# Long-convolution mixer: z weights' low halves to GpSimd, a z unit split around the last sum, a table write on another queue

## The chip, the cores and the metric

The kernel runs on one core of one Trainium2 chip. The metric is the device time of one execution in microseconds. Engines are named as in the profile: PE (TensorE), PEld (its weight loads), DVE (VectorE), ACT (ScalarE), POOL (GpSimd) and SP (SyncE, which here only issues DMAs).

## The reference

The whole reference is a stack of four mixers (long convolution, forgetting attention, short convolution, long convolution) and one block of three attentions and a feed-forward layer, all on 256 positions of 1024 channels in float32. The change touches the long-convolution mixer, which runs first and fourth:

```
def conformer_conv_mixer(h, w_in, conv_w, conv_b, ln_g, ln_b, w_out):
    proj = h @ w_in
    val, glu_gate, z = jnp.split(proj, 3, axis=-1)
    u = val * jax.nn.sigmoid(glu_gate)
    u = causal_depthwise_conv(u, conv_w) + conv_b
    u = jax.nn.silu(layer_norm(u, ln_g, ln_b))
    return (u * jax.nn.silu(z)) @ w_out
```

Here h is 256 x 1024, val, glu_gate and z are 256 x 2048 each, and the convolution has 31 taps on each of 2048 channels. It touches one thing more: a table of relative-position biases that an attention of the last block reads. The kernel builds it at its start and writes it, shifted 16 times, to a DRAM tensor `skew` (28 rows of 16 copies of 384 floats, 0.69 MB), from which it is read at about 1182 us.

## The kernel before

**Units, halves and the ring.** Weights stream from DRAM in units of 256 columns (two halves of 128 columns, 1 MB a unit) through a ring of three buffers. SP issues the loads in order; before it loads unit u it waits until unit u-3 has been used up: by PE for a plain unit, or by the engines that split it for a split unit. A plain unit goes to PE as float32 (L596, in `proj_T`). A split unit is cut into a high part (`whi`, an ACT cast, L362) and a low part (`wlo`, the unit minus its high part, L371 in `lo_to`), and PE forms three products for each tile (L598 to L600). `whi` and `wlo` hold four halves. With the flag `dve` of `unit_in` true, the half with an even number in the whole program has its low part made by DVE and the other by POOL; with the flag false both are POOL's. In the first call of the mixer the even half of a unit is its first, in the second call its second.

**The loop of the mixer.** There are 16 chunks c of 128 channels. `vg` unit c (plain) holds val and gate of chunk c; a `z` unit (split) comes after every fourth of them (z units 0 to 3), and z units 4 to 7 come after the loop. For each chunk ACT applies the sigmoid (L743), DVE multiplies (`gated`, L846) and then does 20 of the 31 taps (L873, L871, L876). ACT multiplies the other 11 taps into four buffers `tmp` (L764) and POOL adds them up (L819, nine adds, and a last one L822 that increments `pool_sum`). ACT may be at most four taps ahead of POOL. DVE joins both parts (`join`, L853 and L854): chunk c-1 is joined after DVE's taps of chunk c, so that POOL has a chunk's time to spare, except for chunk 15, which is joined as soon as DVE's own taps of it and the join of chunk 14 are done. The order on each engine is fixed by the program text. `sigmoid(c+1)`, with the casts that it runs ahead of need (`act_ahead`), stands in chunk c of ACT behind three taps. `conf_z(i)` is SiLU of z unit i with a table load (L728); for i = 0, 1, 2 it stands at the head of `sigmoid` of chunk 4, 8, 12, for i = 3 behind the loop. DVE's low parts stand behind `gated(c+1)` in chunk c, POOL's between its third and fourth add of chunk c. For z unit 3 that is chunk 13, for z unit 4 chunk 14. PE may be at most two units ahead of the engine that empties its bank.

**The statistics.** The layer norm needs the sum (L925, `sum_of`) and the sum of squares (L931, `squares_of`, of squares made by ACT, L749) over all 16 chunks, by PE with a matrix of ones. DVE's first operation on the finished sums is L894. Then come the centring (L900, L915), SiLU (L789), the product with z on POOL (L831) and the output product (L634 to L636), in a fixed interleaving with z units 5 to 7.

**The start.** In the first call POOL also issues the four DMAs of `write_skew` (L797) at the head of its chunk 2. For chunks 0 to 2 a shift is computed and DVE waits for it (L768 on ACT, L886 on DVE) behind ACT's taps of chunk 2.

Of the kernel before, what the change touches and what calls it, by code (L numbers as in the profile page):

```python
# [24 lines left out]
P = 128  # L25
# [4 lines left out]
E = 2048  # L30
# [73 lines left out]
def program(nc, t, out):  # L104
    ctx = ExitStack()
    with ctx:
# [276 lines left out]
        def group(free):  # L383
            groups.append(free)
            return len(groups) - 1
# [34 lines left out]
        def plan_conf(ph, j):  # L420
            w = t["a_w_in"][j]
            n = {"ph": ph, "j": j}
            n["vg"], n["z"] = [], []

            def z_group(i):
                n["z"].append((group((sz_done, j * 8 + i + 1)), unit_in(w, [(2 * E + i * 2 * P, 2 * P)], True)))

            for c in range(KE):

                n["vg"].append((group((u_done, j * KE + c + 1)), unit_in(w, [(c * P, P), (E + c * P, P)], plain=True)))  # L430
                if c % 4 == 3:
                    z_group(c // 4)
            for i in range(4, 8):
                z_group(i)
            n["out"] = plan_out(t["a_w_out"][j], KE)
            return n
# [142 lines left out]
                mm = nc.tensor.matmul(out, ll, rh, start=False, stop=(i == n - 1))  # L579
            return mm  # L580

        def proj_T(pe, g, u, first=False, ph=0):

            b = take_bank(pe, g)
            for a, h in enumerate(hs(u)):
                o = b[:, a * S:(a + 1) * S]
                if is_split(h):
                    split_ready(pe, h)
                    wh, wl = piece(whi, h), piece(wlo, h)
                else:  # L590
                    landed(pe, u)
                for k in range(KD):
                    if first and a == 0:
                        pe.wait_ge(xn_done, 4 * ph + k // 2 + 1)
                    if not is_split(h):
                        mm = nc.tensor.matmul(o, halves[h][1][:, k, :], sqb[:, k, :], start=(k == 0), stop=(k == KD - 1))  # L596
                        continue
                    nc.tensor.matmul(o, wh[:, k, :], xh[:, k, :], start=(k == 0), stop=False)  # L598
                    nc.tensor.matmul(o, wh[:, k, :], xl[:, k, :], start=False, stop=False)  # L599
                    mm = nc.tensor.matmul(o, wl[:, k, :], xh[:, k, :], start=False, stop=(k == KD - 1))  # L600
                mm.then_inc(half_done, 1)
# [129 lines left out]
        def conf_act(act, n):  # L731
# [20 lines left out]
            for c in range(KE):  # L752
                act.wait_ge(u_done, j * KE + c + 1)
                for i in range(TAPS_POOL):
                    if i == TAPS_POOL // 3 and c + 1 < KE:
                        sigmoid(c + 1)
                    if i == 2 * TAPS_POOL // 3 and c >= 3:
                        square(c - 3)
                    k = TAPS_DVE + i
                    m = (j * KE + c) * TAPS_POOL + i  # L760
                    wait(act, tap_done, m - 3)
                    src = up[:, c % 3, k:k + S]
                    bias = cols[:, ROWB + j * KE + c:ROWB + j * KE + c + 1] if i == 0 else 0.0
                    nc.scalar.activation(tmp[:, m % 4, :], src, ACT.Identity, scale=taps[:, j, k, c:c + 1],  # L764
                                         bias=bias).then_inc(tmp_done, 1)
                if c == 2:
                    act.wait_ge(m0_done, j + 1)
                    nc.scalar.activation(shift, bank[2][:, 0:S], ACT.Copy, scale=-1.0 / P).then_inc(shift_done, 1)  # L768
            conf_z(act, n, 3)
            square(KE - 3)  # L770
            act_ahead(act, n["z"][4][1])
            square(KE - 2)
# [16 lines left out]
                nc.scalar.activation(yb[:, c, :], yb[:, c, :], ACT.Silu, scale=lg, bias=lb).then_inc(act_done, 1)  # L789
            out_act(act, n)  # L790

        def write_skew(pool):

            pool.wait_ge(tab_copied, 4)
            for v, (h0, nh) in enumerate(((0, 16), (16, 4), (20, 4), (24, 4))):
                src = tabs[0:nh, v, :].unsqueeze(1).to_broadcast((nh, COPIES, TABLE))
                pool.dma_start(skew[h0:h0 + nh, :, :], src).then_inc(skew_written, 16)  # L797

        def conf_pool(pool, n):
            j = n["j"]  # L800
            for c in range(KE):
                if j == 0 and c == 2:
                    write_skew(pool)
                first = (j * KE + c) * TAPS_POOL
                for i in range(2, TAPS_POOL):
                    if i == TAPS_POOL // 2 and c + 1 < KE:
                        lo_pool_to(pool, ahead(n["vg"][c + 1][1]))
                    to = accp[:, c % 2, i % 2, :]
                    pool.wait_ge(tmp_done, first + i + 1)
                    if i == 2 and c >= 2:  # L810
                        if c < 5:
                            pool.wait_ge(raw_done, 3 * j + c - 1)
                        else:
                            pool.wait_ge(conv_done, j * KE + c - 1)
                    if i >= 4:
                        pool.wait_ge(tap_done, first + (1 if i == 4 else 4 if i == 5 else i - 1))
                    a = tmp[:, (first + i - 2) % 4, :] if i < 4 else to

                    nc.gpsimd.tensor_tensor(to, a, tmp[:, (first + i) % 4, :], ALU.add)\  # L819
                        .then_inc(tap_done, 3 if i == 3 else 1)  # L820
                pool.wait_ge(tap_done, first + TAPS_POOL)
                nc.gpsimd.tensor_tensor(accp[:, c % 2, 0, :], accp[:, c % 2, 0, :], accp[:, c % 2, 1, :], ALU.add).then_inc(pool_sum, 1)  # L822
            lo_pool_to(pool, ahead(n["z"][4][1]))
            for c in range(KE):
                if c in Z_BESIDE:
                    lo_pool_to(pool, ahead(n["z"][Z_BESIDE[c]][1]))
                if c in OUT_BESIDE:
                    lo_pool_to(pool, ahead(n["out"][OUT_BESIDE[c]][2]))
                pool.wait_ge(act_done, j * KE + c + 1)
                wait(pool, sz_done, j * 8 + c // 2 + 1)  # L830
                nc.gpsimd.tensor_tensor(y_slot(pool, n["y0"] + c), yb[:, c, :], zb[:, c, :], ALU.mult).then_inc(y_raw, 1)  # L831
            lo_pool_to(pool, last(n["out"][-1][2]))
# [87 lines left out]
        def conf_pe(pe, n):  # L920
# [24 lines left out]
            for c in range(KE - 4, KE - 2):  # L945
                sum_of(c)
                squares_of(c - 2)
            for c in range(KE - 2, KE):
                sum_of(c)
                squares_of(c - 2)  # L950
            for c in range(KE - 2, KE):
                squares_of(c)
            for i in range(5, 8):
                proj_T(pe, *n["z"][i])
            out_pe(pe, n, y_hi, y_lo, KE, y_split, n["y0"])

# [981 lines left out]
        def _(sp):  # L1938
# [25 lines left out]
            for u, (_, parts) in enumerate(units):  # L1964
                if u >= RING:
# [4 lines left out]
                        wait(sp, lo_pool, n_hi[h] - n_dve(h))  # L1970
                    else:
                        sp.wait_ge(half_done, h + 1)
                for nk, at, width, src in parts:
                    sp.dma_start(raw(u, nk)[:, :, at:at + width], src).then_inc(unit_loaded[u % RING], 16)

# [128 lines left out]
```

## Time and profile before

| | |
|---|---|
| median of 3 runs | 1704.94 us (1703.66 to 1708.4) |
| profiled execution, its own time | 1704.73 us |
| its span in the trace | 1702.9 us |
| first call of the mixer | about 37 to 292 us of the span |
| second call | about 852 to 1098 us |
| PE, DVE, ACT, POOL busy | 94%, 55%, 50%, 44% of the span |
| mean granted TensorE clock | 0.975 |

Times of instructions below are microseconds from the start of the span. In a row of the timeline the bracket is the idle time of that engine just before it, with what ended it. PE's busy share counts overlapping entries, so that its idle time is read from those brackets. Both calls run the same program; from chunk 3 on their rows stand 811.8 us apart, within a microsecond.

### The profile page before, as it was taken

How to read it: one execution, taken by the hardware profiler on the slowest of the kernel's cores; microseconds unless marked ns; L12 is line 12 of the kernel's file. 1: busy time of each engine (PE TensorE's matmuls, PEld its weight loads, DVE VectorE, ACT ScalarE, POOL GpSimd, SP SyncE). 2: the span in 40 equal slices, each digit the busy share in tenths (PEclk: the TensorE clock that was granted, in tenths of full speed). 3: DMA queues.
4: the chain of work that ended last, by engine and by line, in shares of the span. 5: the costliest groups of instructions: out<-in, count | busy, mean ns of one | idle time of the engine just before them, and what ended most of it. 6: DMA issues, size and time to landing. Idle time of an engine off the chain costs nothing.

```text
span 1702.9 us, 28287 instructions
## 1 busy us (share of the span) xinstructions
PE 1593.6 (94%) x10947; PEld 1454.9 (85%) x10947; DVE 934.9 (55%) x2023; ACT 855.7 (50%) x1526; POOL 741.6 (44%) x572
## 2 busy tenths in 40 slices
PE   4999878999999989999899988899999999889998
PEld 3888778998788989999888878898887778889998
DVE  3799965444565554444379998423035545633332
ACT  2577764553455444444357776443325646444442
POOL 0688853332222424444258895365411112334432
PEclk8999989999999999999999999999999999999999
DMA  4654435446553546766444434675752112646654
GB/s 127 143 146 135 130 108 175 133 165 127 122 123 124 163 135 177 195 175 197 124 124 137 136 128 138 152 186 140 182 153 71 51 56 86 194 136 177 187 156 125
DMA packets 341453, 240.11 MB, mean 141 GB/s; under 512 B 36925, under 2 KB 328475, under 8 KB 341320
## 3 DMA queue, kind: packets, MB, share of 16 engines
q1 hardware_dynamic: 329880, 231.33, 47.7%
q10 hardware_dynamic: 10992, 6.29, 1.7%
q0 software_dynamic: 448, 0.69, 0.5%
q8 instruction: 87, 1.43, 0.4%
q14 instruction: 46, 0.38, 0.1%
HBM read 236.55 MB, written 1.74 MB: 140 GB/s over the span
## 4 chain that ended last, share of the span: by engine, by line
PE 70%; DVE 17%; ACT 5%; issue 4%; POOL 2%; DMA 1%; SPq 1%; DVEq 0%; POOLq 0%; ACTq 0%
PE bank L598 8%; DVE bank L876 8%; PE bank L599 8%; PE bank L600 8%; PE bank L634 4%; PE bank L636 4%; PE bank L635 4%; PE bank L990 4%; PE bank L1288 3%; PE bank L596 3%; PE bank L1289 3%; PE bank L1290 3%; PE bank L610 2%; DVE wlo L371 2%; PE bank L1083 1%
## 5 line engine op out<-in xcount | busy, mean ns | idle before, releaser
L371 POOL TENSOR_TENSOR wlo<-ring,whi 128x1024 fp32r<-128x1024 f32 (+3 forms) x210 | 481.7, 2295 | 786.0 <-ACT whi L362 785.9
L362 ACT CAST whi<-ring 128x1024 fp32r<-128x1024 f32 (+4 forms) x389 | 379.2, 990 | 274.8 <-PE bank L600 106.2
L598 PE MATMUL bank<-xh,whi 128*128 128x256 f32 x1384 | 402.4, 291 | 32.4 <-DVE xl L562 19.4
L371 DVE TENSOR_TENSOR wlo<-ring,whi 128x1024 fp32r<-128x1024 f32 (+3 forms) x179 | 254.6, 1423 | 267.0 <-ACT whi L362 266.1
L599 PE MATMUL bank<-xl,whi 128*128 128x256 f32 x1384 | 397.0, 287 | 0.0
L600 PE MATMUL bank<-xh,wlo 128*128 128x256 f32 x1384 | 396.7, 287 | 0.0
L598 PEld LDWEIGHTS bank<-xh,whi 128*128 128x128 f32 x1384 | 271.2, 196 | 42.3 <-issue 39.8
L599 PEld LDWEIGHTS bank<-xl,whi 128*128 128x128 f32 x1384 | 271.6, 196 | 0.2
L600 PEld LDWEIGHTS bank<-xh,wlo 128*128 128x128 f32 x1384 | 271.2, 196 | 0.0
L819 POOL TENSOR_TENSOR scratch<-scratch 128x256 f32<-128x256 f32 x288 | 211.3, 766 | 127.0 <-ACT scratch L764 123.1
L596 PE MATMUL bank<-sqb,ring 128*128 128x256 f32 x1024 | 230.1, 385 | 17.3 <-DVE xl L562 9.7
L596 PEld LDWEIGHTS bank<-sqb,ring 128*128 128x128 f32 x1024 | 196.9, 193 | 47.2 <-issue 10.5
L876 DVE SCALAR_TENSOR_TENSOR bank<-scratch,convw,bank 128x256 f32<-128x256 f32 x576 | 231.1, 482 | 0.0
L764 ACT ACTIVATE scratch<-scratch,convw 128x256 f32<-128x256 f32 x320 | 147.2, 500 | 61.3 <-POOL scratch L819 60.4
L634 PE MATMUL bank<-y_hi,whi 128*128 128x256 f32 x512 | 150.0, 293 | 9.3 <-POOL wlo L371 4.3
L636 PE MATMUL bank<-y_hi,wlo 128*128 128x256 f32 x512 | 147.0, 287 | 0.0
L635 PE MATMUL bank<-y_lo,whi 128*128 128x256 f32 x512 | 146.9, 287 | 0.0
L1288 PE MATMUL bank<-xh,whi 128*128 128x256 f32 x384 | 110.6, 288 | 1.4 <-DVE qk L1251 0.8
L634 PEld LDWEIGHTS bank<-y_hi,whi 128*128 128x128 f32 x512 | 100.5, 196 | 11.7 <-DVE y_lo L714 4.2
L1289 PE MATMUL bank<-xl,whi 128*128 128x256 f32 x384 | 108.6, 283 | 0.0
L1290 PE MATMUL bank<-xh,wlo 128*128 128x256 f32 x384 | 108.5, 283 | 0.0
L635 PEld LDWEIGHTS bank<-y_lo,whi 128*128 128x128 f32 x512 | 100.4, 196 | 0.2
(254 smaller groups left out, 2640.5 us busy)
## 6 DMA issues: line engine op xcount, KB each, us to landing
ring<-in_a_w_in_dram SPq DMA_DIRECT2D x64, 512.0 KB, 5.2
ring<-in_b_w_in_dram SPq DMA_DIRECT2D x32, 1024.0 KB, 5.8
ring<-in_c_w_in_dram SPq DMA_DIRECT2D x64, 512.0 KB, 5.4
ring<-in_w_in_dram SPq DMA_DIRECT2D x26, 1024.0 KB, 5.4
ring<-in_w_ffn_in_dram SPq DMA_DIRECT2D x44, 512.0 KB, 5.1
ring<-in_a_w_in_dram SPq DMA_DIRECT2D x16, 1024.0 KB, 5.3
ring<-in_a_w_out_dram SPq DMA_DIRECT2D x16, 1024.0 KB, 5.0
ring<-in_w_ffn_out_dram SPq DMA_DIRECT2D x16, 704.0 KB, 4.5
```

What stands on the lines that cost most here:

```text
L362: nc.scalar.copy(piece(whi, h)[:, :, 0:n], src).then_inc(hi_done, 1)
L371: engine.tensor_tensor(piece(wlo, h)[:, :, 0:n], src, piece(whi, h)[:, :, 0:n].bitcast(F32), ALU.subtract).then_inc(done, 1)
L596: mm = nc.tensor.matmul(o, halves[h][1][:, k, :], sqb[:, k, :], start=(k == 0), stop=(k == KD - 1))
L598: nc.tensor.matmul(o, wh[:, k, :], xh[:, k, :], start=(k == 0), stop=False)
L599: nc.tensor.matmul(o, wh[:, k, :], xl[:, k, :], start=False, stop=False)
L600: mm = nc.tensor.matmul(o, wl[:, k, :], xh[:, k, :], start=False, stop=(k == KD - 1))
L634: nc.tensor.matmul(o, wh[:, k, :], hi[:, kk, :], start=first, stop=False, skip_group_check=True)
L635: nc.tensor.matmul(o, wh[:, k, :], lo[:, kk, :], start=False, stop=False, skip_group_check=True)
L636: mm = nc.tensor.matmul(o, wl[:, k, :], hi[:, kk, :], start=False, stop=end, skip_group_check=True)
L819: nc.gpsimd.tensor_tensor(to, a, tmp[:, (first + i) % 4, :], ALU.add)\
L876: ins = nc.vector.scalar_tensor_tensor(to[:, a, :], src, w, to[:, a, :], ALU.mult, ALU.add)
L1288: nc.tensor.matmul(o, wh, xh[:, k, :], start=first, stop=False, skip_group_check=True)
```

## The change

Five edits:

1. z units 0, 1, 2, 3 and 5: the flag is false, so POOL makes both low parts. z units 4, 6 and 7 keep one half on DVE.
2. `conf_z(3)` moves from behind ACT's loop into chunk 15, behind three of its 11 taps. It brings the cast of the first half of z unit 5 with it. The `hi_to` that is added behind the taps finds that half cast already.
3. POOL makes the low part of z unit 5's first half directly behind its last chunk; as before, the next halves follow.
4. On PE the first half of z unit 5 comes between the sum of chunk 14 with the squares up to chunk 13 and the sum of chunk 15; the second half comes behind the last squares. The order was: all sums and squares, then the whole unit.
5. `write_skew` is issued by SP, just ahead of the load of `vg` unit 4, instead of by POOL.

```
-                n["z"].append((group((sz_done, j * 8 + i + 1)), unit_in(w, [(2 * E + i * 2 * P, 2 * P)], True)))
+                n["z"].append((group((sz_done, j * 8 + i + 1)), unit_in(w, [(2 * E + i * 2 * P, 2 * P)], i == 4 or i > 5)))
...
-        def proj_T(pe, g, u, first=False, ph=0):
+        def proj_T(pe, g, u, first=False, ph=0, only=(0, 1)):
-            b = take_bank(pe, g)
+            b = take_bank(pe, g) if 0 in only else bank[g % 2]
             for a, h in enumerate(hs(u)):
+                if a not in only:
+                    continue
...
-                    if i == TAPS_POOL // 3 and c + 1 < KE:
-                        sigmoid(c + 1)
+                    if i == TAPS_POOL // 3:
+                        if c + 1 < KE:
+                            sigmoid(c + 1)
+                        else:
+                            conf_z(act, n, 3)
...
+                if c == KE - 1:
+                    hi_to(act, hs(n["z"][5][1])[0])
...
-            conf_z(act, n, 3)
             square(KE - 3)
...
-        def write_skew(pool):
-            pool.wait_ge(tab_copied, 4)
+        def write_skew(sp):
+            sp.wait_ge(tab_copied, 4)
...
-                pool.dma_start(skew[h0:h0 + nh, :, :], src).then_inc(skew_written, 16)
+                sp.dma_start(skew[h0:h0 + nh, :, :], src).then_inc(skew_written, 16)
...
-                if j == 0 and c == 2:
-                    write_skew(pool)
...
+            lo_pool_to(pool, hs(n["z"][5][1])[0])
             lo_pool_to(pool, ahead(n["z"][4][1]))
...
-            for c in range(KE - 2, KE):
-                sum_of(c)
-                squares_of(c - 2)
+            sum_of(KE - 2)
+            squares_of(KE - 4)
+            squares_of(KE - 3)
+            proj_T(pe, *n["z"][5], only=(0,))
+            sum_of(KE - 1)
             for c in range(KE - 2, KE):
                 squares_of(c)
-            for i in range(5, 8):
+            proj_T(pe, *n["z"][5], only=(1,))
+            for i in range(6, 8):
...
+                if u == conf0["vg"][4][1]:
+                    write_skew(sp)
```

## Rows read from the trace of the kernel before

**Rows 1.** The page: busy time, share of the span and instructions of each engine.
```profile
PE 1593.6 (94%) x10947; PEld 1454.9 (85%) x10947; DVE 934.9 (55%) x2023; ACT 855.7 (50%) x1526; POOL 741.6 (44%) x572
```

**Rows 2.** The chain that ended last, first call: start, length, what.
```profile
80.54 3.59 DVE bank L876 x10
...
152.53 7.17 PE bank L596 x32
```

**Rows 3.** Timeline of DVE, first call, chunk 13 and behind the loop.
```profile
179.63 1.72 DVE L371 TENSOR_TENSOR wlo<-ring,whi 128x1024 fp32r<-128x1024 f32 x1
...
206.07 4.52 DVE L371 TENSOR_TENSOR wlo<-ring,whi 128x1024 fp32r<-128x1024 f32 x2
210.51 0.41 DVE L894 TENSOR_SCALAR rr<-bank 128x256 f32<-128x256 f32 x1
```

**Rows 4.** Timeline of PE, first call; the bracket is idle time before.
```profile
73.41 7.07 PE L596 MATMUL bank<-sqb,ring 128*128 128x256 f32 x32
...
82.67 7.17 PE L596 MATMUL bank<-sqb,ring 128*128 128x256 f32 x32 [1.75 <-ACT wide L728]
...
189.03 0.59 PE L931 MATMUL bank<-scratch,cst 128*128 128x256 f32 x2
...
205.12 1.22 PE L925 MATMUL bank<-wide,cst 128*128 128x256 f32 x2 [4.47 <-DVE wide L854]
```

**Rows 5.** Waits of PE, first call, 90 to 160: total us, times, longest.
```profile
PE bank L596 <- DVE scratch L846: 3.0, 2, 2.1
PE bank L598 <- DVE wlo L371: 0.6, 1, 0.6
```

**Rows 6.** Timeline of POOL, first call, chunks 13 and 15.
```profile
177.90 2.37 POOL L371 TENSOR_TENSOR wlo<-ring,whi 128x1024 fp32r<-128x1024 f32 x1
...
197.65 6.24 POOL L819 TENSOR_TENSOR scratch<-scratch 128x256 f32<-128x256 f32 x9
203.96 0.73 POOL L822 TENSOR_TENSOR scratch<-scratch 128x256 f32<-128x256 f32 x1
```

**Rows 7.** POOL's adds by tile, 174 to 206: duration ns min/median/max.
```profile
L819 POOL TENSOR_TENSOR scratch<-scratch x27: 721/733/1724, 174.7 to 203.2; 128x256 f32<-128x256 f32 x27
```

**Rows 8.** Timeline of ACT, first call: sigmoid of chunk 4, and chunk 15.
```profile
83.93 0.39 ACT L743 ACTIVATE scratch<-bank 128x256 f32<-128x256 f32 x1
...
196.20 0.51 ACT L764 ACTIVATE scratch<-scratch,convw 128x256 f32<-128x256 f32 x1 [0.19 <-POOL scratch L819]
...
201.84 1.03 ACT L362 CAST whi<-ring 128x1024 fp32r<-128x1024 f32 x1
202.89 1.28 ACT L728 ACT_TABLE_LOAD   x1
204.18 0.60 ACT L728 ACTIVATE wide<-bank 128x512 f32<-128x512 f32 x1
```

**Rows 9.** Timeline of POOL, first call: issue of the table write.
```profile
72.06 2.56 POOL L797 DMA_DIRECT2D skew<-qk  x4
```

**Rows 10.** Timeline of SP's queue, first call: issue of `vg` unit 4's load.
```profile
60.31 0.99 SPq L1974 DMA_DIRECT2D ring<-in_a_w_in_dram  x2
```

**Rows 11.** DMA issues, 70 to 76: what, count, KB each, median us to landing.
```profile
skew<-qk POOLq DMA_DIRECT2D x1, 384.0 KB, 5.8
skew<-qk POOLq DMA_DIRECT2D x3, 96.0 KB, 15.0
```

**Rows 12.** The chain, second call: matmuls at the two clock levels.
```profile
1049.35 0.21 PE bank L635
...
1055.01 0.12 PE bank L635
```

**Rows 13.** Timelines of DVE and POOL, second call.
```profile
891.34 0.75 DVE L886 TENSOR_TENSOR wide<-wide,bank 128x256 f32<-128x256 f32 x2 [0.35 <-ACT bank L768]
...
1015.73 0.73 POOL L822 TENSOR_TENSOR scratch<-scratch 128x256 f32<-128x256 f32 x1
...
1021.55 0.42 DVE L894 TENSOR_SCALAR rr<-bank 128x256 f32<-128x256 f32 x1 [1.69 <-PE bank L931]
```

## The prediction

> **What bounds the kernel now.** The page first: PE is busy 94% of the span and DVE 55% [rows 1], so an engine at half load can matter only in a stage where the others wait for it. The chain of waits shows where: in the first call it runs on DVE's taps from 80.54 us to near 150, touches PE at 152.53 [rows 2], and then changes between PE, ACT and POOL until 205. The second call reads alike. So the loop looks bound by DVE; the question is how far behind it the others are.
>
> PE: from 152.53 (four `vg` units and z unit 3, with their sums) it works without a wait until 189.5 [rows 2, 4], 36.9 us for four chunks. In the first call it waited only 2.1 us before `vg` unit 8, 0.9 before `vg` unit 12 (3.0 in two waits, the longest 2.1) and 0.6 for a DVE low part in between [rows 5]. So four chunks of DVE with one low part take 36.9 + 0.9 = 37.8 us, and PE is 0.9 behind.
>
> POOL: the sum of chunk 15 ends at 203.96 + 0.73 = 204.69 [rows 6], which I call T. PE sums chunk 14 at 205.12, after a wait for the join of chunk 14, which ended at about 205.0 [rows 4]; the join of chunk 15 follows directly. So at the end of the loop POOL is within half a microsecond of DVE. In chunk 15 it has no chunk to spare. This small distance decides more than DVE's load.
>
> After T: DVE's first operation on the statistics, which I call S, is at 210.51 in the first call, T + 5.8 [rows 3, 6], and at 1021.55 in the second, T + 5.1 with T = 1015.73 + 0.73 [rows 13]. Everything that follows is ordered behind S: normalising, SiLU, the products, and in between the casts and low parts of z units 6 and 7 that PE waits for. So a shift of S is taken as a shift of the end of the call, and a shift of T is one of S.
>
> **The change, step by step** (plus is later).
>
> *Low parts of z units 1 to 3.* DVE loses about 1.7 us for each [rows 3], 5.1 per call. But PE permits only part: over a cycle of four chunks 0.9 instead of 1.7. POOL gains a low part of 2.37 [rows 6] and loses something: one of its adds takes 1.72 instead of 0.73 [rows 7], just where DVE's low part runs beside it, at 179.63 to 181.35 [rows 3, 7]. So POOL pays 2.37 - 0.99 = +1.4 for each. Away from the end POOL has a chunk to spare. In chunk 13 it hasn't: with chunks 13, 14 and 15 it runs straight to T. There: +1.4.
>
> The Trainium skill (SBUF - State Buffer, section "Who interferes with whom") says that a DVE instruction with two SBUF inputs and a GpSimd instruction that reads SBUF block each other for a whole instruction. The 1.72 of the trace agrees with it. By it POOL's price would be 2.37 less up to 1.7, so +0.7 instead of +1.4.
>
> *`conf_z(3)` in chunk 15.* Behind ACT's third tap (ends 196.7) come a cast of 1.03, a table load of 1.28 and SiLU of 0.60 [rows 8], 2.9 in all; the fourth tap ends at about 200.0, where POOL's second add used to start at 197.65 + 0.7 = 198.35 [rows 6]. So +1.65 on T. That SiLU's set also serves the taps is taken from the loop, where no load stands between them; else 1.3 more. Behind the loop ACT has 2.9 less to do, which hid beside PE: worth nothing.
>
> *The start.* POOL's chunk 1 gets +1.4 for z unit 0. In the first call its chunk 2 loses the 2.56 of the DMA issues [rows 9]: together -1.2, and DVE waits for ACT and POOL there. In the second call nothing is removed: DVE's wait was 0.35 [rows 13] and it would itself be earlier, so +1.4 less a little, +1.3.
>
> *The table write on SP's queue.* The load of `vg` unit 4 was issued at 60.31 [rows 10] and PE used it from 73.41 [rows 4]. Now four writes stand ahead of it. Before, they were issued from 72.06, and three of them took 15.0 us to land [rows 11]: 16 from first issue to last landing. The load now lands between 60.3 + 13.7 = 74 (the write's last bytes overlap with the load) and 60.3 + 16 + 3.7 = 80 (nothing overlaps, a load's bytes behind it). I take the middle, 77. Then PE is idle 3.6 us, and begins `vg` unit 4 at the low clock, as after the 4.47 idle before 205.12, when a sum took twice its time [rows 4]: +1.6. PE ends it at about 86.0 instead of 80.9, and `vg` unit 5 starts at 86.0 instead of 82.67, +3.3. ACT's sigmoid of chunk 4 was at 83.93 [rows 8], now 86.0: +2.1 there and about +1.7 for DVE.
>
> *Sum up to T.* First call: before `vg` unit 8 PE is at 3.3 - 2.1 - 0.6 = +0.6, DVE at 1.7 - 1.7 = 0: PE decides. Before unit 12 PE is at 0.6 - 0.9 = -0.3, DVE at -1.7. Chunk 13 of POOL hangs on PE's unit 13, so -0.3, and T is at -0.3 + 1.4 + 1.65 = +2.7. With the table write hidden the same walk from -1.2 gives -2.9 at unit 8 and -3.8 at unit 12, so T = -0.8; with a landing at 80, +5.7. Second call: from +1.3, -0.4 at unit 8, -1.3 at unit 12, so T = +1.7, with bounds of 0 and +3.
>
> *From T to S.* PE now does z unit 5's first half before the last sum. Its low part begins at T on POOL: 2.37, and up to 1.0 more if DVE's low part of z unit 6 blocks it. Then 24 matmuls, at 0.12 or 0.21 each [rows 12]: 2.9 or 5.1. Then a sum and two squares, 0.43 each at the high clock (0.59 less what overlaps [rows 4]) or 0.85: 1.3 or 2.6. With 0.1 for the hand-over, S is at T + 6.7 to T + 11.2. PE is idle ahead of T as before (4.47), so I take the low clock for the half and the high one behind it: 2.37 + 0.1 + 5.1 + 1.3 = T + 8.9. First call 8.9 - 5.8 = +3.1 (from +0.9 to +5.4), second 8.9 - 5.1 = +3.8 (from +1.6 to +5.1). What DVE saves (the 4.52 of two low parts becomes one [rows 3]) is hidden by this. That PE has half a unit less to do behind S is worth nothing: it waits there for ACT's and POOL's casts and low parts of z units 6 and 7.
>
> Sum: 2.7 + 3.1 + 1.7 + 3.8 = +11.3. The profiled execution took 1704.73, the median is 1704.94; both give 1716.
>
> **Rivals.**
>
> *The write is hidden and the half runs at the high clock:* -0.8 + 0.9 + 1.7 + 1.6 = +3.4, 1708. For it: the load had 7 us of slack. Against it: the 15.0 us.
>
> *Faster:* DVE stays the bound because POOL catches up. It decides if POOL ends its sum of chunk 15 at least 2.4 us before DVE's joins, so that the low part of the half is ready at the join. Then T would be -1.2 - 5.1 in the first call, +1.3 - 5.1 in the second, S stays where it is behind T: -10, 1695. Against it: POOL is within 0.5 us of DVE now and its chunks 13 and 15 get longer.
>
> *The three small writes one after another,* not side by side: each of the second and third adds most of 10 us more, PE starts `vg` unit 4 near 95, and the first call is some 15 us later still: about 1732. Each of the three reads only four partitions; in the trace they ran together, so this isn't seen. The Trainium skill (DMA: Bandwidth & Descriptors, section "Why a DMA increments its semaphore by 16 and not by 1") has a rule that would bring it about: writes of four rows issued by SP all go to the same lowest-numbered four DMA engines, those issued by GpSimd to the next ones in turn; no run here shows it.
>
> **How the numbers follow.** Forecast (POOL's end and the half before the last sum make it slower, the write partly exposed): 0.62, its own range 1710 to 1723. Hidden write and high clock, 1708: 0.18. Faster, 1695: 0.12. Writes in series: 0.08. Leaving out the faster case and most of the series case, the range is 1702 to 1724. About 0.3% (5.1 us) is what a measurement tells from no change. Slower by more: 0.62 + 0.08, 0.70; the 1708 case lies within, 0.18; faster 0.12.
>
> **What would show it.** In the profile after: POOL's L822 of chunk 15 no earlier than 204 in the first call and 1017 in the second, relative to their starts; DVE idle before the join of chunk 15, waiting for L822; PE waiting for POOL's `wlo` before the first half of z unit 5; S at T + 7 to 11; PE idle before `vg` unit 4 with `ring` late. The prediction is wrong if DVE still has no idle time before the last join, if PE has z unit 5's low part at hand when chunk 14 is joined, or if L596 at about 73.4 starts on time: then the first rival's terms apply.

## The result, and the profile after

After the change the kernel takes 1720.78 us (median of 4 runs, 1718.25 to 1721.86), beside 1706.67 us for the kernel before in all of its 4 runs so far (1703.66 to 1708.59). The ratio is 1.0082, with an interval of 1.006 to 1.0104: slower, by 14 us. The profiled execution took 1721.85 us, its span is 1720.0, 17.1 more than before.

The page, busy time of each engine, and the chain of work that ended last by engine:

```profile
PE 1601.1 (93%) x10947; PEld 1461.6 (85%) x10947; DVE 916.6 (53%) x2013; ACT 855.1 (50%) x1526; POOL 754.1 (44%) x578
...
PE 76%; DVE 8%; ACT 6%; issue 4%; POOL 3%; SPq 1%; DMA 1%; ACTq 0%; DVEq 0%; POOLq 0%
```

Beside [rows 1] DVE has 18.3 us less to do and POOL 12.5 more. That is what the change does, and it says nothing of the end. Two marks of each call do: T, the end of POOL's sum of chunk 15, and S, the start of DVE's first operation on the statistics. Here both are counted from the reciprocal of the normalisation ahead of the call (L558 on DVE, at 33.46 and 847.39 us in the trace of before, 33.53 and 858.06 after), so that what happened earlier in the kernel drops out.

| us | before | after | more |
|---|---|---|---|
| first call: T | 171.2 | 178.0 | +6.8 |
| first call: T to S | 5.8 | 9.2 | +3.4 |
| first call: to the next stage's L558 | 259.7 | 269.8 | +10.1 |
| second call: T | 169.1 | 171.2 | +2.1 |
| second call: T to S | 5.1 | 8.4 | +3.3 |
| second call: to the next stage's L558 | 252.4 | 257.0 | +4.6 |
| the attention stages, from there to the last L558 | 398.8 | 401.4 | +2.6 |

**Where the first call's 6.8 us come from.** SP's queue and PE, around the load of `vg` unit 4 (before: [rows 10, 4]):

```profile
60.45 8.35 SPq L803 DMA_DIRECT2D skew<-qk  x4
68.84 7.70 SPq L1984 DMA_DIRECT2D ring<-in_a_w_in_dram  x2
```

```profile
81.25 9.49 PE L598 MATMUL bank<-sqb,ring 128*128 128x256 f32 x32 [7.75 <-DMA ring<-in_a_w_in_dram]
```

The chain of work in that stretch (start, length, what) names each step:

```profile
60.45 0.69 SPq L803
...
61.18 0.70 SPq L803
...
61.92 3.08 SPq L803
...
65.04 3.76 SPq L803
...
68.84 3.69 SPq L1984
...
72.58 8.53 DMA ring<-in_a_w_in_dram
```

POOL issued the same four DMAs in 2.56 us [rows 9]. On SP the first two are short, and then each issue takes 3 to 4 us, the load's own two included (3.69 and 3.96). The view by windows says why. Its columns are the window, its length, busy time (and instructions) of PE, PEld, DVE, ACT and POOL, the granted clock, the share of the 16 DMA engines that was busy, and GB/s:

```profile
62.00:65.00 3.00, 3.00 (x15) 2.65 (x14) 3.00 (x9) 2.50 (x7) 2.43 (x3) 1.00 0.90 102
66.00:69.00 3.00, 3.00 (x21) 2.79 (x20) 2.96 (x9) 0.00 (x0) 3.00 (x3) 1.00 0.22 26
```

```profile
65.00:69.00 4.00, 4.00 (x25) 3.68 (x24) 3.93 (x11) 0.03 (x1) 4.00 (x3) 1.00 0.31 36
69.00:73.00 4.00, 4.00 (x36) 4.00 (x35) 2.34 (x7) 3.00 (x7) 3.92 (x7) 1.00 0.24 30
73.00:77.00 4.00, 0.50 (x5) 0.29 (x3) 3.87 (x10) 2.84 (x7) 4.00 (x7) 0.85 0.58 123
77.00:81.00 4.00, 0.00 (x0) 0.00 (x0) 3.06 (x9) 3.77 (x8) 3.92 (x7) 0.50 0.82 239
```

From 62 to 65 us the large write (384 KB, from 16 partitions) moves 102 GB/s. From 66 to 69 the share is 0.22, which is 3.6 of 16 DMA engines, and 26 GB/s move (from 69 to 73 an instruction fetch on another queue raises the figures to 0.24 and 30). The three small writes are 96 KB each, [rows 11], which at 26 GB/s is 3.8 us each. That is about the length of one held issue, and three of them, 11.4 us, reach from the large write's end near 65.6 to about 77. So the reading is that they run one behind the other on about four DMA engines, and that SP is held in its issues meanwhile. PE ran out of work at 73.5, and at 77 it is at 0.50 of its clock, the 1.2 GHz level; its `vg` unit 4 then takes 9.49 us instead of 7.07.

**Where the 3.3 us from T to S come from.** PE, POOL and DVE in the first call (before: [rows 4, 6, 3]):

```profile
206.52 1.22 PE L930 MATMUL bank<-wide,cst 128*128 128x256 f32 x2 [3.71 <-DVE wide L859]
...
213.98 0.55 PE L600 MATMUL bank<-xh,whi 128*128 128x256 f32 x1 [3.61 <-POOL wlo L371]
...
219.19 0.59 PE L930 MATMUL bank<-wide,cst 128*128 128x256 f32 x2
```

```profile
205.22 5.51 POOL L823 TENSOR_TENSOR scratch<-scratch 128x256 f32<-128x256 f32 x8 [1.76 <-ACT scratch L769]
210.81 0.73 POOL L826 TENSOR_TENSOR scratch<-scratch 128x256 f32<-128x256 f32 x1
211.49 5.66 POOL L371 TENSOR_TENSOR wlo<-ring,whi 128x1024 fp32r<-128x1024 f32 x2
```

```profile
205.59 0.42 DVE L858 TENSOR_TENSOR wide<-bank,scratch 128x256 f32<-128x256 f32 x1
...
211.63 0.42 DVE L858 TENSOR_TENSOR wide<-bank,scratch 128x256 f32<-128x256 f32 x1 [5.17 <-POOL scratch L826]
...
212.61 2.30 DVE L371 TENSOR_TENSOR wlo<-ring,whi 128x1024 fp32r<-128x1024 f32 x1
220.76 0.42 DVE L899 TENSOR_SCALAR rr<-bank 128x256 f32<-128x256 f32 x1 [5.84 <-PE bank L936]
```

DVE joins chunk 14 at 205.59 and then stands idle for 5.17 us until POOL's last sum (T = 211.54). PE stands idle for 3.61 until POOL has the low part of z unit 5's first half, at 213.98 it begins that half, and only at 219.19 does it sum chunk 15, whose join was ready at 212.5. So the last sum starts 6.7 us after its join is ready, behind 24 matmuls that nobody needs yet. The second call shows the same:

```profile
1029.36 0.42 DVE L858 TENSOR_TENSOR wide<-bank,scratch 128x256 f32<-128x256 f32 x1 [5.13 <-POOL scratch L826]
...
1037.65 0.42 DVE L899 TENSOR_SCALAR rr<-bank 128x256 f32<-128x256 f32 x1 [7.41 <-PE bank L936]
```

### The profile page after: what moved, and what is told of

Same layout as the page of the kernel before. It is cut to its first block, busy times and chain, and to the rows that moved or that the text cites. A ratio compares the mean times of both kernels' runs of the same rounds, so it can differ in the third digit from the quotient of the medians.

```text
span 1720.0 us, 28288 instructions
## 1 busy us (share of the span) xinstructions
PE 1601.1 (93%) x10947; PEld 1461.6 (85%) x10947; DVE 916.6 (53%) x2013; ACT 855.1 (50%) x1526; POOL 754.1 (44%) x578
## 4 chain that ended last, share of the span: by engine, by line
PE 76%; DVE 8%; ACT 6%; issue 4%; POOL 3%; SPq 1%; DMA 1%; ACTq 0%; DVEq 0%; POOLq 0%
PE bank L598 9%; PE bank L600 9%; PE bank L601 8%; PE bank L602 8%; PE bank L636 4%; PE bank L638 4%; PE bank L637 4%; PE bank L998 4%; PE bank L1296 3%; PE bank L1297 3%; PE bank L1298 3%; PE bank L612 2%; ACT whi L362 2%; POOL scratch L823 1%; PE bank L1091 1%
## 5 line engine op out<-in xcount | busy, mean ns | idle before, releaser
L371 POOL TENSOR_TENSOR wlo<-ring,whi 128x1024 fp32r<-128x1024 f32 (+3 forms) x220 | 505.5, 2302 | 785.2 <-ACT whi L362 784.9
L602 PE MATMUL bank<-xh,wlo 128*128 128x256 f32 x1384 | 399.1, 288 | 0.0
L371 DVE TENSOR_TENSOR wlo<-ring,whi 128x1024 fp32r<-128x1024 f32 (+3 forms) x169 | 236.4, 1399 | 269.4 <-ACT whi L362 268.6
L823 POOL TENSOR_TENSOR scratch<-scratch 128x256 f32<-128x256 f32 x288 | 202.9, 738 | 128.6 <-ACT scratch L769 128.4
```

The source lines that it names most:

```text
L371: engine.tensor_tensor(piece(wlo, h)[:, :, 0:n], src, piece(whi, h)[:, :, 0:n].bitcast(F32), ALU.subtract).then_inc(done, 1)
```

## The experiments

Each was run beside the kernel before on the same chip. T and S are as above, first call / second call, from one profile of each kernel.

| run | median us | ratio to before | T | T to S |
|---|---|---|---|---|
| after | 1720.78 | 1.0082 [1.006, 1.0104] | 178.0 / 171.2 | 9.2 / 8.4 |
| e1: after, write on POOL | 1714.8 | 1.005 [1.0036, 1.0064] | 173.4 / 171.0 | 8.6 / 8.3 |
| e2: after, z unit 5 whole | 1710.08 | 1.0032 [1.002, 1.0045] | 178.0 / 170.5 | 4.1 / 3.6 |
| e3: after, SiLU behind the loop | 1716.07 | 1.006 [1.0047, 1.0073] | 175.9 / 168.9 | 8.5 / 8.5 |
| e4: after, z unit 3 shared | 1716.16 | 1.0063 [1.005, 1.0076] | 176.2 / 169.9 | 7.3 / 8.9 |
| e5: before, write on SP | 1712.16 | 1.0037 [1.0025, 1.0049] | 177.8 / 169.2 | 5.9 / 5.1 |
| e6: before, split alone | 1709.81 | 1.0026 [1.0018, 1.0035] | 171.2 / 169.3 | 7.8 / 7.9 |
| e7: before, other placement | 1698.49 | 0.9956 [0.9944, 0.9968] | 165.9 / 167.1 | 5.7 / 4.4 |
| e8: before, loop part alone | 1699.08 | 0.9966 [0.9953, 0.9978] | 165.8 / 167.0 | 5.8 / 4.9 |
| e9: after, write behind the load | 1714.18 | 1.005 [1.0034, 1.0066] | 170.6 / 171.2 | 9.2 / 8.4 |
| e10: e7, z unit 6's low part later | 1695.93 | 0.9948 [0.9934, 0.9961] | 165.9 / 166.9 | 4.2 / 5.2 |
| e11: e1 and e2 together | 1705.48 | 0.9999 [0.9991, 1.0008] | 173.3 / 171.2 | 4.1 / 3.0 |

### One part of the change undone (e1 to e4)

**e1**, the write issued by POOL again:

```
-                if u == conf0["vg"][4][1]:
-                    write_skew(sp)
...
+                if j == 0 and c == 2:
+                    write_skew(pool)
```

> The changed kernel with one part undone: the table is again written from GpSimd's queue at the head of its chunk 2. T is the end of POOL's last sum in a call, S DVE's first operation on the finished sums, both counted from DVE's first reciprocal of the call. Main theory (the write stands ahead of the load of vg unit 4, PE idles 7.8 us and runs that unit at the low clock): PE does not wait for the ring before vg unit 4, T of the first call falls from 178.0 to about that of a call without the write, 173.5, S from 187.2 to 182.5; the whole is 4 to 5 us less than the changed kernel, about 1716. The second call does not move. Rival (the write is hidden behind the slower chain of POOL, and the wait before unit 4 costs nothing by chunk 15): T of the first call stays near 178, the time near 1720.

T came back by 4.6 us in the first call and by next to nothing (0.2) in the second; by the ratios the kernel is 0.0032 shorter, 5.5 us (the two intervals touch, 1.0064 and 1.006). `vg` unit 4 was on time in PE:

```profile
74.49 7.17 PE L598 MATMUL bank<-sqb,ring 128*128 128x256 f32 x32
```

So the write on SP's queue is the first call's largest term, and the mechanism is the late load. T is still 2.2 us later than before, as in the second call (1.9 here).

**e2**, z unit 5 whole, behind all sums:

```
-            proj_T(pe, *n["z"][5], only=(0,))
             sum_of(KE - 1)
...
-            proj_T(pe, *n["z"][5], only=(1,))
-            for i in range(6, 8):
+            for i in range(5, 8):
```

> The changed kernel with PE's order of before: all sums and squares first, then z unit 5 whole. Main theory (the last sum and squares wait behind the half of z unit 5, which waits for POOL's low part): T stays in both calls (178.0 and 171.2 from the call's start), S comes at T + 3 to 4 instead of T + 9.2 and T + 8.4, since the join of chunk 14 is long done and only one sum and two squares are left behind T; 5 to 6 us less in each call, 10 to 11 in all, about 1710. Rival (the half only fills time in which the squares wait for ACT, and S is set by DVE's low part and ACT's squares): S moves by 1 to 2, the time stays within 3 us of 1720.

T stayed (178.0, and 170.5 for 171.2), and S came to T + 4.1 and T + 3.6, 5.1 and 4.8 us less. DVE, first call:

```profile
211.85 0.42 DVE L858 TENSOR_TENSOR wide<-bank,scratch 128x256 f32<-128x256 f32 x1 [5.17 <-POOL scratch L826]
...
212.83 2.31 DVE L371 TENSOR_TENSOR wlo<-ring,whi 128x1024 fp32r<-128x1024 f32 x1
215.83 0.42 DVE L899 TENSOR_SCALAR rr<-bank 128x256 f32<-128x256 f32 x1 [0.70 <-PE bank L936]
```

DVE now makes its one low part and finds the statistics 0.70 us behind it. The half ahead of the last sum costs 9.9 us by the marks and 8.5 by the ratios (1.0082 less 1.0032), the largest part of the whole. That is more than the 3.4 and 3.3 of the table above, because without the split S would have come 1.7 and 1.5 us nearer to T than before. In the first call it was DVE's two low parts that set T + 5.8, [rows 3], and one of them is gone. In the second call of before DVE had one low part there and then waited 1.69 us for PE, [rows 13], which had the sums of chunk 14 and of chunk 15 behind T; now chunk 14's are done by T, because T comes 5 us after DVE is ready.

**e3**, the cast and SiLU of z unit 3 behind ACT's loop, and **e4**, a half of z unit 3 on DVE:

```
# e3
-                    if i == TAPS_POOL // 3:
-                        if c + 1 < KE:
-                            sigmoid(c + 1)
-                        else:
-                            conf_z(act, n, 3)
+                    if i == TAPS_POOL // 3 and c + 1 < KE:
+                        sigmoid(c + 1)
...
-                if c == KE - 1:
-                    hi_to(act, hs(n["z"][5][1])[0])
...
+            conf_z(act, n, 3)
# e4
-  ... unit_in(w, [(2 * E + i * 2 * P, 2 * P)], i == 4 or i > 5)))
+  ... unit_in(w, [(2 * E + i * 2 * P, 2 * P)], i in (3, 4) or i > 5)))
```

> The changed kernel with SiLU of z unit 3 (conf_z(3)) behind ACT's loop again. Main theory (the cast, the table load and the SiLU inside chunk 15 hold up ACT's fourth tap and with it POOL by 1.65 us): T is 1.6 to 1.8 earlier in both calls, S follows, since PE waits for POOL's low part after T: 3.3 less in all, about 1717.5. Rival (DVE or PE, not POOL, sets T): T does not move. Rival (ACT is too busy behind the loop with it, so that the squares become late): T moves but S does not.

> The changed kernel with z unit 3 shared between DVE and POOL again (flag true), z units 0, 1, 2, 5 as changed. Main theory (from chunk 13 on POOL runs straight to T, and a second low part there costs it 2.37 less the 1.0 that it loses beside DVE's low part): T is 1.4 earlier in both calls, S follows, 2.8 less in all, about 1718; DVE's idle time before the last join falls by about 3. Rival by the lock rule taken fully (0.7 per low part): 1.4 less in all. Rival (POOL has time to spare): T stays.

T came back by 2.1 and 2.3 us with e3, by 1.8 and 1.3 with e4; the ratios by 0.0022 and 0.0019, 3.8 and 3.2 us. The intervals of these ratios overlap with that of after, so the reading rests on T, which moved in both calls. Both say the same of chunks 13 to 15: POOL runs straight to T there, and what ACT or POOL gets more to do arrives at T. With e3, ACT's work between its third and fourth tap is gone. In the trace of after it reads as ACT and the gap on POOL:

```profile
201.74 1.03 ACT L362 CAST whi<-ring 128x1024 fp32r<-128x1024 f32 x1
202.79 1.28 ACT L730 ACT_TABLE_LOAD   x1
204.09 0.60 ACT L730 ACTIVATE wide<-bank 128x512 f32<-128x512 f32 x1
204.58 0.90 ACT L769 ACTIVATE scratch<-scratch,convw 128x256 f32<-128x256 f32 x2
```

No table load stands ahead of the taps at 204.58, as the prediction had taken from the loop. In e4 DVE's idle time before the last join fell from 5.17 to 1.45 us, and the first call's T to S from 9.2 to 7.3, which was not expected. There PE had been idle for only 0.81 us ahead of the half, the granted clock was 1.00 from 211 to 214, and the half took 2.95 us:

```profile
210.82 0.36 PE L600 MATMUL bank<-xh,whi 128*128 128x256 f32 x1 [0.81 <-POOL wlo L371]
```

### One part alone in the kernel before (e5, e6)

**e5** is the write on SP's queue in the kernel before, the same two edits as in the change's diff:

> The kernel before with the table write alone moved to SP's queue, ahead of the load of vg unit 4. T and S as in the earlier runs (from DVE's first reciprocal of the call; before: T 171.2, S 177.0, second call 169.1 and 174.2). Main theory (the load is 8 us late for PE, PE runs the unit at the low clock, ACT's sigmoid of chunk 4 and DVE's product wait, and DVE, the bound from there on, never gets it back): DVE's product of chunk 4 is some 6 us later than before, T and S of the first call 5 to 6.5 later, the second call unchanged; 1711 to 1712. Rival (in the changed kernel the delay of 4.6 was a meeting of two changes, POOL's extra low part and the late load; alone it is less than 3): within 1706 to 1709.

SP's queue, and PE:

```profile
59.28 8.36 SPq L797 DMA_DIRECT2D skew<-qk  x4
```

```profile
79.82 9.58 PE L596 MATMUL bank<-sqb,ring 128*128 128x256 f32 x32 [7.29 <-DMA ring<-in_a_w_in_dram]
```

Alone, the write moves T by +6.6 us in the first call and by nothing in the second: the same 8.4 us of issue, and the same idle time in PE. The median is 6.7 higher. So none of it needs the other edits. That is more than the 4.6 that e1 takes back: behind the late load the other edits make T only 0.2 later (178.0 beside 177.8), and without it 2.2 (173.4 beside 171.2). That fits the prediction's walk, in which DVE's missing low parts make up lateness of the loop, but it isn't tested by itself.

**e6** is the split alone: z unit 5 wholly on POOL, its first half ahead of the last sum.

```
-  ... unit_in(w, [(2 * E + i * 2 * P, 2 * P)], True)))
+  ... unit_in(w, [(2 * E + i * 2 * P, 2 * P)], i != 5)))
...
+            lo_pool_to(pool, hs(n["z"][5][1])[0])
             lo_pool_to(pool, ahead(n["z"][4][1]))
...
+            proj_T(pe, *n["z"][5], only=(0,))
+            sum_of(KE - 1)
```

> The kernel before with two parts alone: both low parts of z unit 5 by POOL directly behind its last chunk, and PE's order of the changed kernel (the first half of z unit 5 ahead of the sum of chunk 15). Main theory (the half waits for its low part until T + 2.5, runs 5 us at the low clock, and the last sum stands behind it): T unchanged in both calls, S at T + 8.5 to 9.2 instead of T + 5.8 and T + 5.1, so 3 to 3.5 later in each call; 1712 to 1713. Rival (with DVE and POOL ending together, the half costs only what the rest of PE's queue then saves): S at T + 6 to 7, 1707 to 1709.

T stayed; S was at T + 7.8 and T + 7.9: between the two expectations. PE and the clock, first call:

```profile
203.97 1.22 PE L928 MATMUL bank<-wide,cst 128*128 128x256 f32 x2 [4.47 <-DVE wide L857]
204.98 1.91 PE L934 MATMUL bank<-scratch,cst 128*128 128x256 f32 x4
206.34 0.78 PE L600 MATMUL bank<-xh,whi 128*128 128x256 f32 x1
```

```profile
206.00:208.00 2.00, 2.00 (x13) 1.82 (x12) 2.00 (x1) 1.73 (x3) 2.00 (x1) 0.71 0.00 0
```

The low part came about as the sums of chunk 14 ended, so PE had no second gap, and the clock rose to 2.4 GHz within the half's first microsecond (0.71 is the mean of the stretch; the matmuls are 0.21 us apart up to 207.1 and 0.12 behind). In the kernel after, PE stands idle for 3.61 us just before the half and does all of it at 1.2 GHz in the first call: 5.2 us instead of 3.4, and 2.95 in e4. How long a half takes hangs on what PE did before it.

### The same means in another place (e7, e8, e10)

The loop edits shorten DVE's path; what cost was where their work went. **e8** keeps z units 0 and 3 shared as before, gives only units 1 and 2 to POOL, where POOL has a chunk to spare, and issues the write from POOL behind its loop. **e7** gives it z unit 5 too, without a split, and takes the sums as they come.

```
# e8
-  ... unit_in(w, [(2 * E + i * 2 * P, 2 * P)], True)))
+  ... unit_in(w, [(2 * E + i * 2 * P, 2 * P)], i not in (1, 2))))
...
-                if j == 0 and c == 2:
-                    write_skew(pool)
...
             lo_pool_to(pool, ahead(n["z"][4][1]))
+            if j == 0:
+                write_skew(pool)
# e7: as e8, but
+  ... unit_in(w, [(2 * E + i * 2 * P, 2 * P)], i not in (1, 2, 5))))
...
-            for c in range(KE - 2, KE):
-                sum_of(c)
-                squares_of(c - 2)
+            squares_of(KE - 4)
+            sum_of(KE - 2)
+            squares_of(KE - 3)
+            sum_of(KE - 1)
```

> As e7_balanced, but only its part in the loop: z units 1 and 2 on POOL and the table write behind POOL's loop; z unit 5 shared and all sums in the order of before. Main theory: T as in e7_balanced (166 and 167), S at T + 5.8 and T + 5.1 as before; 5 earlier in the first call, 2 in the second, 7 in all, about 1699. Rival (POOL, with two more low parts in the loop, sets T): T no earlier than 170 and 169, within 1 of the kernel before.

> A kernel made from the findings, from the kernel before: z units 1 and 2 wholly on POOL (it has a chunk to spare there), z unit 0 and 3 shared as before, z unit 5 wholly on POOL, PE's sums as before but with the squares of chunk 12 ahead of the sum of chunk 14, and the table write issued by POOL behind its last low parts, where it idles. Main theory: first call T 166 (PE bound before vg units 8 and 12, so 5.1 earlier), S at T + 4 to 4.5, 6 to 7 earlier than before; second call T 167, S 171.3, 3 earlier; 9 to 10 in all, about 1696. Rival (the time after S fills up whatever is won before it, since loads of z units 6 and 7 and of the output are then late): S moves, the ends of the calls don't, above 1702.

Both are faster than before, by 6.4 and 7.0 us in the median. T moved by -5.4 and -5.3 in the first call and by -2.1 and -2.0 in the second. Only the second call shows the low parts by themselves: in the first, the write has left POOL's chunk 2 as well. POOL is ahead of DVE's join now (its last sum in e8 ends at 197.84, DVE's last join begins at 198.24 without a wait). e7 adds nothing that can be told apart: DVE's single low part beside POOL's took 3.35 us,

```profile
200.88 3.35 DVE L371 TENSOR_TENSOR wlo<-ring,whi 128x1024 fp32r<-128x1024 f32 x1 [1.07 <-ACT whi L362]
```

and with the wait for ACT's cast ahead of it filled the room that the other left.

**e10** is e7 with DVE's low part of z unit 6's first half behind the statistics instead of ahead of them (the `dve_ahead` that stands there, which runs ahead of need as far as z unit 6, is dropped; the part is made in its later turn):

```
             dve.wait_ge(conv_done, j * KE + KE)
-            dve_ahead(dve, n["z"][4][1])
             dve.wait_ge(mean_done, j + 1)
```

> e7_balanced with one thing more: DVE makes the low part of z unit 6's first half no longer between the last join and the statistics, but with its next ones, behind the reciprocal of the layer norm. Theory (in the first call of e7_balanced that low part, 3.35 us beside POOL's own, set S at T + 5.7 where the second call, without it, had T + 4.4): S of the first call at T + 4.3 to 4.6, 1.1 to 1.4 earlier, second call unchanged, the end of the first call earlier by the same, about 1697. Rival (PE then waits for that low part before z unit 6, and the bank comes late): S earlier, the end of the call not.

```profile
203.69 0.42 DVE L893 TENSOR_SCALAR rr<-bank 128x256 f32<-128x256 f32 x1 [2.95 <-PE bank L930]
...
209.19 1.22 DVE L371 TENSOR_TENSOR wlo<-ring,whi 128x1024 fp32r<-128x1024 f32 x1
```

The first call's T to S fell from 5.7 to 4.2. The second's rose from 4.4 to 5.2, although DVE has no low part there in either kernel and the instructions between T and S are the same: in e7 the granted clock is 1.00 from 1013 us on, before the last squares are done, and in e10 it stays at 0.50 past them. So 0.8 us of T to S can differ between two profiles without an edit. The median is 1695.93, the fastest measured here, 9.4 us below before. Its interval overlaps that of e7 (0.9944 to 0.9968), so that this last edit brings anything is not shown; that the placement as a whole does is.

### Place in the queue, and what is left of the gain (e9, e11)

**e9** leaves the write on SP's queue, but directly behind the load of `vg` unit 4:

```
-                if u == conf0["vg"][4][1]:
-                    write_skew(sp)
                 for nk, at, width, src in parts:
                     sp.dma_start(raw(u, nk)[:, :, at:at + width], src).then_inc(unit_loaded[u % RING], 16)
+                if u == conf0["vg"][4][1]:
+                    write_skew(sp)
```

> The changed kernel with the table write on SP's queue directly behind the load of vg unit 4 instead of directly ahead of it. Theory (it is the place in the queue that costs, not the queue or the write's share of the DMA engines): PE does not wait for the ring before vg unit 4; the loads of vg units 5 and 6 come behind the write, needed 9 and 17 us later, so they are late by 0 to 3; T of the first call 170 to 173 (changed kernel 178.0, with the write on GpSimd 173.4), 5 to 8 us less than the changed kernel, 1711 to 1715. Rival (the write delays whatever is loaded next by its full 8 us, and PE is as late at vg unit 5 as it was at 4): PE waits 5 or more before vg unit 5, T stays above 175.

```profile
60.19 0.99 SPq L1982 DMA_DIRECT2D ring<-in_a_w_in_dram  x2
61.23 8.38 SPq L803 DMA_DIRECT2D skew<-qk  x4
```

```profile
83.30 7.15 PE L598 MATMUL bank<-sqb,ring 128*128 128x256 f32 x32 [2.46 <-DMA ring<-in_a_w_in_dram]
```

The four issues still take 8.38 us from first to last, but `vg` unit 4 is in time and PE waits for unit 5 only, 2.46 us, which the loop makes up: T is 170.6, 7.4 less than after. So it is the place ahead of a load with 7 us of slack that costs, not SP's queue. Beside e1, where POOL issues the write, T is 2.8 us earlier, about the 2.56 us that POOL no longer spends on issuing it, [rows 9]. So the 4.6 of e1 read as 7.4 for the late load less 2.8.

**e11** undoes both large parts, the write (e1) and the order on PE (e2), and keeps the rest.

> The changed kernel with both large terms undone together: the table write from GpSimd as before, and PE's sums ahead of the whole z unit 5. What stays of the change: low parts of z units 0 to 3 and 5 on POOL, SiLU of z unit 3 in chunk 15. Theory (the terms add): first call T 173.4, S at T + 4.1, 177.5; second call T 170.5, S 174.1; both S within 0.6 of the kernel before (177.0 and 174.2), so 1705 to 1707. Rival (a term that shows only when both are gone, such as DVE's saved 5 us): 1702 or less.

0.9999 [0.9991, 1.0008], over 12 runs: no difference. T is 2.1 us later than before in both calls, and T to S 1.7 and 2.1 shorter. What S gains on T (one low part less on DVE, and chunk 14's sums done by T), POOL and ACT pay for ahead of T. Here the gain that the change could have had went.

## Why the prediction was right, by its steps

**The second call's T and the loop.** Forecast +1.7, measured +2.1. DVE waits for POOL's L826 at the last join (5.13 us), as foreseen; before, it didn't. Undone one by one, the low part in chunk 13 gave 1.8 and 1.3 us (forecast 1.4) and the work of ACT in chunk 15 gave 2.1 and 2.3 (forecast 1.65). Why the latter is 0.45 and 0.65 above its forecast stays open.

**The first call's T** was mis-sized: forecast +2.7, measured +6.8. The failing term is the landing of `vg` unit 4's load, taken at 77 us, "the middle" between 74 and 80. It landed at 81.1. The rest of the walk holds: with the write hidden it gave -0.8, and e9, which hides all but 2.46 us, has -0.6. The upper bound had assumed that the load's bytes come behind the write's, and that is what happened: the windows of after show the DMA engines' share at 0.23 once more, as for the small writes alone, before the rest of the load moves (that those four engines are the ones that the load still lacked is read from this, not measured by itself):

```profile
76.00:77.00 1.00, 0.00 (x0) 0.00 (x0) 0.87 (x3) 1.00 (x3) 1.00 (x3) 0.50 0.23 23
...
78.00:79.00 1.00, 0.00 (x0) 0.00 (x0) 1.00 (x3) 0.92 (x2) 1.00 (x2) 0.50 1.02 305
```

With T = +5.7 for a landing at 80 and 1.1 more for the lateness, +6.8 follows. The wait of PE was 7.75 instead of 3.6, the low clock cost 2.4 instead of 1.6. What the working had not seen is that SP itself would be held: the issues took 8.35 us, so that the load's first DMA was issued only at 72.5. How much of the last 1.1 us that hold makes isn't separated. The lower bound's 13.7 us come from no row. The 16 us for the whole write were read from a median, 15.0; by single landings the write took 17.9 in before, 72.06 to 89.98. A middle between two bounds was no estimate; what decided was whether the load shares the write's DMA engines and gets its turn beside it, and of that before had no row.

**From T to S.** Forecast T + 8.9 in both calls, measured 9.2 and 8.4. By its terms: low part 2.37 and hand-over 0.1, measured 2.44 (211.54 to 213.98); the half 5.1, measured 5.2 and 4.35 (in the second call the clock rose to 2.4 GHz at about 1035, inside the half); sum, squares and hand-over 1.3, measured 1.6. This part was right in mechanism and size, and e2 shows what it costs against the order that it could have had: 5.1 and 4.8.

**Behind S** nothing was to change. In the first call +10.2 at S is +10.1 at the end; in the second +5.4 is +4.6, so 0.8 came back.

**The sum.** Forecast 1716 (+11.3), measured +14.1 in the medians and +17.1 in the profiled spans. The two calls account for 14.7 (10.1 + 4.6). So the forecast lies within its range although one term was 4.1 us short: the other terms were within 0.5, 0.8 came back behind S, and the range was wide enough. That the sum came this near is in part luck. Another 2.6 stand in the attention stages, which the change doesn't touch. There one stretch at 1.2 GHz is longer; by windows, before and after:

```profile
1172.00:1179.00 7.00, 7.00 (x63) 6.90 (x63) 6.96 (x31) 0.00 (x0) 1.00 (x1) 0.76 0.48 151
```

```profile
1187.00:1197.00 10.00, 10.00 (x75) 9.90 (x75) 9.97 (x45) 1.04 (x1) 1.20 (x1) 0.66 0.34 106
```

0.24 / 0.5 of 7 us are 3.4 us at half clock, 0.34 / 0.5 of 10 us are 6.8. Half of the 3.4 more is lost, 1.7 of the 2.6 us; the other 0.9 stay unexplained. The experiments fall into the same two groups, whatever was edited: these stages took 398.8 to 399.1 us in before, e5, e7 and e11, and 400.9 to 402.3 in all others. Why one profile gets the longer stretch stays open, and a difference of 2 us between two kernels' single profiles is not to be explained by their edits.

**The rivals.** A hidden write and a high clock in the half (1708) is refuted by PE's wait of 7.75 and by the 5.2 us of the half. Faster (1695) needed POOL to end 2.4 us before DVE's joins; POOL ended 5 us after DVE was ready. That e10 was measured at 1695.93 doesn't bear it out: it gets there by other edits, with POOL given only what it has room for. The small writes one after another (1732, chance 0.08) came true as a mechanism and not as a price: in after their queue, SP's, fills 22.6% of the DMA engines from 69 to 73 us. Issued by POOL in e8, in a stretch in which nothing else moves (210.5 to 213.5), they fill 68.4%, nearly 11 of 16. The DMA view of after and of e8 (queue, packets, MB, share of 16 engines):

```profile
q1 hardware_dynamic: 71, 0.10, 22.6%
```

```profile
q0 software_dynamic: 16, 0.07, 68.4%
```

The Trainium skill says (DMA: Bandwidth & Descriptors, "Why a DMA increments its semaphore by 16 and not by 1") that a write of four rows uses four DMA engines, from SP always the lowest-numbered ones, from GpSimd the next in turn. The trace agrees in the count, 3.6 for one write at a time and nearly 11 for three at once; which engines they are it doesn't show. The rival's price was wrong because it gave each write the 10 us and more that it takes side by side with the others from POOL, [rows 11]. In series from SP each took under 4 us. In all, the two ways move 26 and 25 GB/s, so the three take about as long in series as side by side. That is why a time taken from POOL's trace nearly fitted SP's queue.

## What to carry to other kernels

Work moved off the engine that seems to bind is free only while the engine that takes it has slack before its next deadline: a low part more cost 1.3 to 1.8 us in the third chunk from the end of the loop, and two of them gave 2.1 us where POOL had a chunk to spare (the second call of e8). Filler work doesn't belong ahead of the last small step of the chain (a sum of 0.59 us and two of squares, 1.03, here) if it waits for another engine itself; it costs its wait, its length and the clock that the wait loses, however busy it makes PE. And a DMA moved to another queue costs by what stands behind it there: price it by the rate at which it moves on any queue (here 26 GB/s), not by the time of its issue on the old one, and put it behind the load that is needed next.

## What was not expected of the hardware

- **An issue on SP can take as long as the transfer in front of it.** Two DMAs of a `vg` unit are issued in 0.99 us [rows 10]. Behind writes that read four partitions each, one issue took 3.08 to 3.96 us in after; the write's four took 8.35, 8.36 and 8.38 in three kernels (0.7 to 1.04 each for the first two). The same four took POOL 2.56 [rows 9]. In before, with no write on SP's queue, one issue of a load, at 80.93, took 7.70 us while POOL's writes were under way. The Trainium skill (DMA: Bandwidth & Descriptors, "Issuing engines are not separate DMA queues") says that the sequencer's time to initiate a DMA is "usually small relative to the DMA itself", and here it was as large.
- **The write's rate went with the partitions that it reads, on either queue.** From SP, 102 GB/s from 16 partitions at 90% of the DMA engines, 26 from four at 22%. From POOL, 25 GB/s from four partitions each, with three writes at once on some 11 DMA engines. So three times the engines moved no more; the loads on the same 16 reached 305 GB/s (78 to 79 us in after). Why the rate goes with the partitions no run here separates.
- **DVE and POOL on SBUF.** The same low part took DVE 1.22 us in e10, where no low part of POOL ran beside it, 2.30 in after and 3.35 in e7. POOL's first low part behind T takes 2.34 us; in after it began at 211.49 and ended at 213.83, so DVE's, begun at 212.61 and ended at 214.91, had 1.1 us of its own behind that end. In e7 POOL's two end at 203.15 and DVE's at 204.23, 1.1 behind. The Trainium skill (SBUF — State Buffer, "Who interferes with whom") calls this an exclusive lock on a shared port; DVE's length reads as the rest of POOL's instruction and then its own, which agrees.
